# Retention states of sample batches: row groups of two batches, four 32-row updates, states by key halves

## The reference

```python
scores = jnp.einsum('bihd,bjhd->bhij', q, k) * mask[None]
inner = jnp.einsum('bhij,bjhe->bihe', scores, v)
cross = jnp.einsum('bihd,bhde->bihe', q, S) * q_dec[None, :, :, None]
S_new = (jnp.exp(log_g * C)[None, :, None, None] * S
         + jnp.einsum('bjhd,bjhe->bhde', k * k_dec[None, :, :, None], v))
return S_new, inner + cross
```

## Time and profile before

| | us |
|---|---|
| median of three timed runs (2913.4 to 2915.48) | 2915.39 |
| the profiled execution | 2908.85 |
| its span, first to last instruction | 2907.1 |
| TensorE busy | 2885.7 (99%) |
| VectorE busy | 1566.3 (54%) |
| ScalarE busy | 1121.1 (39%) |

### The profile page before, as it was taken

One profiled execution on the slowest core, in us unless ns is written; L12 is line 12 of the kernel. 1 busy time (PEld: TensorE's weight loads), 2 busy tenths in 40 slices (PEclk: granted clock), 3 DMA queues, 4 the chain that ended last, 5 costly groups with the idle time before them and its releaser, 6 DMA issues.

```text
span 2907.1 us, 57564 instructions
## 1 busy us (share of the span) xinstructions
PE 2885.7 (99%) x24818; PEld 2808.3 (97%) x24818; DVE 1566.3 (54%) x1695; ACT 1121.1 (39%) x1129; POOL 112.9 (4%) x144
## 2 busy tenths in 40 slices
PE   9999999999999999999999999999999999999998
PEld 9999999999999999898998999999999999999998
DVE  6444444444567566676765655465544444444444
ACT  5333333333334453444534644333433333333333
POOL 0000000000000002012020010000000000000000
PEclk9999999999999999999999999999999999999999
DMA  5444454444456543635436544555444444444444
GB/s 207 160 166 157 160 171 171 164 168 151 162 182 229 188 179 109 241 121 204 164 127 245 175 142 162 196 200 186 162 164 161 162 160 169 173 161 171 151 160 142
DMA packets 85461, 495.80 MB, mean 171 GB/s; under 512 B 10320, under 2 KB 10496, under 8 KB 44096
## 3 DMA queue, kind: packets, MB, share of 16 engines
q1 hardware_dynamic: 71424, 444.14, 43.2%
q0 software_dynamic: 9280, 32.70, 3.1%
q10 hardware_dynamic: 4608, 16.78, 1.4%
HBM read 462.78 MB, written 30.80 MB: 170 GB/s over the span
## 4 chain that ended last, share of the span: by engine, by line
PE 94%; DVE 3%; ACT 1%; DMA 1%; issue 0%; SPq 0%; DVEq 0%; ACTq 0%
PE psum L529 29%; PE psum L530 29%; PE psum L531 29%; PE psum L874 1%; PE psum L705 1%; DVE sb_w_lo L1486 1%; PE psum L695 1%; DVE sb_w_lo L1480 0%; PE psum L726 0%; DMA sb_raw<-in_w_wo 0%; PE psum L650 0%; ACT sb_w_hi L1066 0%; PE psum L884 0%; PE psum L887 0%; PE psum L945 0%
## 5 line engine op out<-in xcount | busy, mean ns | idle before, releaser
L529 PE MATMUL psum<-sb_h_hi,sb_w_hi 128*128 128x288 f32 x4384 | 1305.5, 298 | 3.0 <-DVE sb_w_lo L1480 1.5
L530 PE MATMUL psum<-sb_h_lo,sb_w_hi 128*128 128x288 f32 x4384 | 1294.2, 295 | 0.0
L531 PE MATMUL psum<-sb_h_hi,sb_w_lo 128*128 128x288 f32 x4384 | 1294.1, 295 | 0.0
L1486 DVE TENSOR_TENSOR sb_w_lo<-sb_raw,sb_w_hi 128x2048 fp32r<-128x2048 f32 (+1 forms) x348 | 712.4, 2047 | 724.5 <-ACT sb_w_hi L1066 721.5
L1066 ACT ACTIVATE sb_w_hi<-sb_raw 128x2048 fp32r<-128x2048 f32 (+1 forms) x349 | 600.2, 1720 | 1247.2 <-PE psum L531 1211.9
L529 PEld LDWEIGHTS psum<-sb_h_hi,sb_w_hi 128*128 128x128 f32 x4384 | 822.8, 188 | 19.7 <-issue 11.3
L530 PEld LDWEIGHTS psum<-sb_h_lo,sb_w_hi 128*128 128x128 f32 x4384 | 823.7, 188 | 2.5 <-issue 1.0
L531 PEld LDWEIGHTS psum<-sb_h_hi,sb_w_lo 128*128 128x128 f32 x4384 | 823.3, 188 | 0.0
L529 PE MATMUL psum<-sb_g_hi,sb_w_hi 128*128 128x288 f32 x1408 | 416.8, 296 | 0.7 <-DVE sb_w_lo L1486 0.5
L530 PE MATMUL psum<-sb_g_lo,sb_w_hi 128*128 128x288 f32 x1408 | 416.5, 296 | 0.0
L531 PE MATMUL psum<-sb_g_hi,sb_w_lo 128*128 128x288 f32 x1408 | 414.0, 294 | 0.0
(11 more groups left out here) (379 smaller groups left out, 2435.8 us busy)
## 6 DMA issues: line engine op xcount, KB each, us to landing
sb_raw<-in_gu SPq DMA_DIRECT2D x175, 1024.0 KB, 4.8
sb_raw<-in_down SPq DMA_DIRECT2D x128, 704.0 KB, 4.0
sb_raw<-in_w_mix SPq DMA_DIRECT2D x72, 1024.0 KB, 4.8
sb_raw<-in_w_gates SPq DMA_DIRECT2D x32, 1024.0 KB, 5.3
sb_s_ret<-in_s_ret POOLq DMA_DIRECT2D x32, 512.0 KB, 7.6
out_ret_s<-sb_s_ret ACTq DMA_DIRECT2D x32, 512.0 KB, 3.1
sb_raw<-in_w_ro SPq DMA_DIRECT2D x16, 1024.0 KB, 4.8
sb_raw<-in_w_out SPq DMA_DIRECT2D x16, 1024.0 KB, 4.8
```

The source lines that it names most:

```text
L529: pe.matmul(out, wh, xh, start=start, stop=False)
L530: pe.matmul(out, wh, xl, start=False, stop=False)
L531: return pe.matmul(out, wl, xh, start=False, stop=stop)
L1486: dve.tensor_tensor(w_lo[:, slot, 0:cols], raw[:, slot, 0:cols], w_hi[:, slot, 0:cols].bitcast(F32), ALU.subtract).then_inc(lo_made, 2)
```

## The change

The state slots no longer hold a batch each. A slot holds one key half of two batches, and the host permutes the states to fit. The sample's tokens are taken in four row groups of 32 rows: two batches of 4 tokens, four times over (three as high and low parts, the fourth zero). VectorE makes these repeated strips of values and keys first (`vs_rep`, `ks_rep`, step "gathered"), TensorE turns them by six ordinary turns of 128 columns instead of 18 narrow products, and factors by row (in `rc`) make high and low parts when they are copied out. An `update` is then four products of 32 rows, one for each row group and PSUM bank, for one key half of four batches; VectorE adds two batches' key half at once (128 x 1024). The output sums of the two halves are added by VectorE, so the fold is half as long. The sample's inner product takes split scores (`sc_3`) in one pass. The gaps have new weights. Left out in the diff: sizes and places of tiles, the names of steps, `cross` (its slot is now `2 * e + j // 2`), the splitting of `scores`, the waits' values, and the constants.

```diff
@@ -84,8 +84,8 @@
-RET_GAPS = (("turned", 2.6), ("scores", 4.2), ("kv_s0", 1.1), ("kv_s1", 1.1), ("kv_s2", 1.1), ("kv_s3", 1.4), ("kv1", 6.2),
-            ("kv_s4", 1.1), ("kv_s5", 1.1), ("kv_s6", 1.1), ("o_turned", 2.2), ("summed", 1.4), ("norm", 0.6))
+RET_GAPS = (("turned", 2.6), ("scores", 3.0), ("kv_s0", 0.8), ("kv_s1", 2.2), ("kv_s2", 2.2), ("kv1", 6.2),
+            ("kv_s3", 0.8), ("kv_s4", 2.2), ("kv_s5", 0.9), ("o_turned", 2.2), ("summed", 1.4), ("norm", 0.6))
@@ -663,10 +662,9 @@
+                after(ret_dve, RET_DVE, "gathered")
...
-                    for n in range(3):
-                        mm = pe.matmul(psum[n * NS:(n + 1) * NS, 5, m * P:(m + 1) * P], vg[:, 0, m, SEQ:T], ident[:, :],
-                                       start=True, stop=True)
+                    mm = transpose(psum[:, 5, m * P:(m + 1) * P], vs_rep[:, m, :])
@@ -676,43 +674,47 @@
-                    pe.matmul(psum[0:NS, 7, P:P + NS], qk[:, 2 + e, SEQ:T], qk[:, e, SEQ:T], start=(e == 0),
+                    pe.matmul(psum[:, 7, P:P + NS], ks_rep[:, e, :], qk[:, e, SEQ:T], start=(e == 0),
...
-                    for n in range(3):
-                        mm = pe.matmul(psum[n * NS:(n + 1) * NS, 4, e * P:(e + 1) * P], qk[:, 2 + e, SEQ:T], ident[:, :],
-                                       start=True, stop=True)
+                    mm = transpose(psum[:, 4, e * P:(e + 1) * P], ks_rep[:, e, :])
...
-                def update(half, bb, banks):
-                    for e in range(2):
-                        u = 2 * (bb - SLOTS * half) + e
-                        if u >= 3:
-                            pe.wait_ge(s_new, h * (2 * SB) + (2 * SLOTS * half + u - 2))
-                        step(pe.matmul(psum[:, banks[u % 3], :], k_own[:, bb % SLOTS, e * P:(e + 1) * P], v_3[:, :],
-                                       start=True, stop=True))
-                after(ret_dve, RET_DVE, "k_owned0")
+                def update(half, e):
+                    for j in range(SLOTS):
+                        rows = slice(j * NS, (j + 1) * NS)
+                        mm = pe.matmul(psum[:, 4 + j, :], k_own[rows, half, e * P:(e + 1) * P], v_3[rows, :], start=True, stop=True)
+                    step(mm)
+                after(ret_dve, RET_DVE, "masked")
...
-                for bb in range(SLOTS):
-                    update(0, bb, (6, 7, 4))
-                    weave(f"ret_kv_s{bb}")
-                pe.wait_ge(s_new, h * (2 * SB) + 2 * SLOTS - 2)
+                weave("ret_kv_s0")
...
+                after(ret_dve, RET_DVE, "k_owned")
+                pe.sem_inc(parted, 1)
+                update(0, 0)
+                weave("ret_kv_s1")
+                pe.wait_ge(s_new, h * SB + 2)
+                pe.sem_inc(parted, 1)
+                update(0, 1)
+                weave("ret_kv_s2")
+                pe.wait_ge(s_new, h * SB + 3)
@@ -729,21 +731,21 @@
+                pe.matmul(psum[0:NS, 6, :], sc_3[:, :], v_3[:, :], start=True, stop=False, skip_group_check=True)
+                cross(1, 6)
+                weave("ret_kv_s3")
+                after(ret_act, RET_ACT, "state1")
+                after(ret_dve, RET_DVE, "o_s_added")
...
-                pe.matmul(psum[0:NS, 6, :], scores[0:NS, 384:384 + NS], v_tok_s[:, :], start=True, stop=False,
-                          skip_group_check=True)
-                cross(1, 6)
-                after(ret_act, RET_ACT, "state1")
-                after(ret_dve, RET_DVE, "k_owned1")
-                for bb in range(SLOTS, SB):
-                    update(1, bb, (7, 4, 5))
-                    if bb < SB - 1:
-                        weave(f"ret_kv_s{bb}")
-                after(ret_act, RET_ACT, "o_s1")
+                update(1, 0)
+                weave("ret_kv_s4")
+                pe.wait_ge(s_new, h * SB + 6)
+                pe.sem_inc(parted, 1)
+                update(1, 1)
+                weave("ret_kv_s5")
+                pe.wait_ge(s_new, h * SB + 7)
...
-                    for half in range(2):
-                        mm = pe.matmul(psum[:, 6, m * NS:(m + 1) * NS], o_s[half][:, m * P:(m + 1) * P], rc[:, C_FOLD:RC],
-                                       start=(half == 0), stop=(half == 1), skip_group_check=True)
+                    mm = pe.matmul(psum[:, 4, m * NS:(m + 1) * NS], o_s[:, m * P:(m + 1) * P], rc[:, C_FOLD:RC], start=True, stop=True)
@@ -1262,24 +1264,28 @@
-                ch.do(act.activation(v_3[:, :], psum[0:3 * NS, 5, :], ACT.Copy), wait=False)
-                step(act.activation(v_tok_s[:, :], psum[0:NS, 5, :], ACT.Copy))
+                step(act.activation(v_3[:, :], psum[:, 5, :], ACT.Copy, scale=rc[:, C_V1:C_V1 + 1]))
...
-                ch.do(act.activation(k_s[:, :], psum[0:3 * NS, 4, 0:256], ACT.Copy, scale=rc[0:3 * NS, C_KD + 2:C_KD + 3]))
-                step(act.activation(k_3[:, :], k_s[:, :], ACT.Copy))
+                for half in range(2):
+                    ins = act.activation(k_own[:, half, :], psum[:, 4, 0:DK], ACT.Copy, scale=rc[:, C_KA0 + half:C_KA0 + half + 1])
+                    step(ins) if half else ch.do(ins, wait=False)
...
-                step(act.activation(o_s[0][:, :], psum[:, 5, :], ACT.Copy))
-                for bb in range(SLOTS):
-                    send(bb)
-                    weave(f"ret_kv_s{bb}")
+                step(act.activation(o_s[:, :], psum[:, 5, :], ACT.Copy))
+                weave("ret_kv_s0")
+                send(0)
+                send(1)
+                weave("ret_kv_s1")
+                send(2)
+                send(3)
+                weave("ret_kv_s2")
@@ -1287,12 +1293,13 @@
-                after(ret_pe, RET_PE, "cross1")
-                step(act.activation(o_s[1][:, :], psum[:, 6, :], ACT.Copy))
-                for bb in range(SLOTS, SB):
-                    if bb < SB - 1:
-                        weave(f"ret_kv_s{bb}")
-                    send(bb)
+                weave("ret_kv_s3")
+                weave("ret_kv_s4")
+                send(4)
+                send(5)
+                weave("ret_kv_s5")
+                send(6)
+                send(7)
@@ -1807,6 +1814,13 @@
+                mixed_in(dve, h, 7)
+                do(dve.tensor_copy(vs_rep[:, :, :].rearrange("p m (g c u) -> p m g c u", c=4, u=2 * ST),
+                                   vg[:, 0, :, SEQ:T].rearrange("p m (g u) -> p m g u", u=2 * ST).unsqueeze(3).broadcast_to(
+                                       [P, VT, 4, 4, 2 * ST])), wait=False)
+                step(dve.tensor_copy(ks_rep[:, :, :].rearrange("p m (g c u) -> p m g c u", c=4, u=2 * ST),
+                                     qk[:, 2:4, SEQ:T].rearrange("p m (g u) -> p m g u", u=2 * ST).unsqueeze(3).broadcast_to(
+                                         [P, 2, 4, 4, 2 * ST])))
@@ -1814,43 +1828,46 @@
-                step(dve.tensor_tensor(v_3[NS:2 * NS, :], psum[NS:2 * NS, 5, :], v_3[NS:2 * NS, :].bitcast(F32), ALU.subtract))
+                step(dve.scalar_tensor_tensor(out=v_3[:, :], in0=psum[:, 5, :], scalar=rc[:, C_V2:C_V2 + 1],
+                                              in1=v_3[:, :].bitcast(F32), op0=ALU.mult, op1=ALU.add))
...
-                rest = slice(2 * NS, 3 * NS)
-                step(dve.tensor_tensor(k_3[rest, :], k_s[rest, :], k_3[rest, :].bitcast(F32), ALU.subtract))
-                after(ret_dve, RET_DVE, "k_parts")
-                def own_keys(half):
-                    b = slice(SLOTS * half, SLOTS * (half + 1))
-                    step(dve.tensor_tensor(k_own[:, :, :], k_3[:, :].bitcast(F32).unsqueeze(1).broadcast_to([3 * NS, SLOTS, DK]),
-                                           own[0:3 * NS, b].unsqueeze(2).broadcast_to([3 * NS, SLOTS, DK]), ALU.mult))
-                own_keys(0)
+                for half in range(2):
+                    ins = dve.scalar_tensor_tensor(out=k_own[:, half, :], in0=psum[:, 4, 0:DK],
+                                                   scalar=rc[:, C_KB0 + half:C_KB0 + half + 1],
+                                                   in1=k_own[:, half, :].bitcast(F32), op0=ALU.mult, op1=ALU.add)
+                    step(ins) if half else do(ins, wait=False)
...
-                def state_s(half, bb, banks):
-                    for e in range(2):
-                        after(ret_pe, RET_PE, f"kv_s{bb}" + "eo"[e])
-                        u = 2 * (bb - SLOTS * half) + e
-                        dve.scalar_tensor_tensor(out=s_ret[:, bb % SLOTS, e, :], in0=s_ret[:, bb % SLOTS, e, :],
-                                                 scalar=rc[:, C_KD + 3:C_KD + 4], in1=psum[:, banks[u % 3], :], op0=ALU.mult,
-                                                 op1=ALU.add).then_inc(s_new, 1)
-                for bb in range(SLOTS):
-                    state_s(0, bb, (6, 7, 4))
-                    weave(f"ret_kv_s{bb}")
-                own_keys(1)
+                def states(half, e):
+                    after(ret_pe, RET_PE, f"kv_s{half}{e}")
+                    for pr in range(2):
```

(50 more changed lines are left out.)

33 lines of the change are left out of this document (16 added, 17 removed).

## The result

The change makes the kernel slower: 2930.47 us (median of 5 runs, 2930.21 to 2931.77) against 2914.14 for the kernel before on the same chip (5 runs), a ratio of 1.0056, 95% interval [1.0042, 1.0071], +16.3. The forecast was 2936.5 with a range of 2924 to 2945. The profiled execution has a span of 2928.8, +21.7 over the 2907.1 of before; forecast for that comparison was +21.2.

What follows compares the result with a forecast made beforehand. TensorE, busy 99% of the span, was taken as the bound. Savings −17.0, holes +25.2, state waits +4.2 and clock +8.8 gave +21.2, 2930.0 profiled; with 6.5 to the median, 2936.5, range 2924 to 2945.

Steps and rivals of the forecast that it cites:

- value turns: TensorE, start of each head: four plain turns replace 12 products of 32 columns, 0.44 against 1.00, −0.56 a head.
- scores: TensorE, scores in each head: four instructions and two turns, 0.66 against 0.68, no change.
- updates: TensorE, state updates: four groups on four strips at 0.40 replace 16 products, 1.6 against 3.7, −2.1 a head.
- sample's scores times values: TensorE, the sample's own scores times values: two passes of 0.97 become one of 0.235, −0.74 a head.
- fold: TensorE, fold after the last updates: 16 instructions, 1.87 long, become 8, −0.85 a head.
- holes: TensorE waits for VectorE's copies before its turns: 6.0 in heads two to four, 7.1 in the first, +25.2.
- waits for states: TensorE waits for VectorE's state operations: 0.1 after a half's first group, 1.3 before the fold in three heads, +4.2 together.
- clock behind the holes: TensorE at half rate after each hole: 2.2 lost per hole, bounds 0 and 2.8, +8.8 for four.
- The third rival: Second cross products: state stores and loads come late, up to 1.2 a head, 2941.3; chance 0.08.
- From the profiled execution to the median: Whole kernel: the timed median lies 6.5 above the profiled execution; added to the change, 2930.0 profiled becomes 2936.6.
- The rival of an undisturbed clock: TensorE behind the holes: the clock stays up, or falls in one head only, 8.8 less, 2927.8; chance 0.22.

Runs made afterwards that it cites:

- double groups: The changed kernel with every group of four updates issued twice into the same banks, 16 groups more: 2935.98 us, one run.
- filled holes: The changed kernel with 46 (first head 54) turns of a constant matrix before each wait for the copies: 2928.8 us, ratio 1.0051.
- the version with the pieces from another gap: The change with copies moved ahead and woven pieces taken from before the first cross products, put before fold and second cross products: 2905.34 us, ratio 0.9968.

## Why the prediction was right, and where its terms were off

The side, the place and the mechanism came as forecast: four holes before the turns of the repeated values, released by VectorE's copy of the keys, a fall of the clock behind each, a wait before the fold in heads one to three. Term by term, in the profiled executions, four heads together:

| term | forecast | measured |
|---|---|---|
| value turns | −2.2 | −3.0 |
| scores | 0 | −1.0 |
| updates | −8.4 | −4.9 |
| sample's scores times values | −3.0 | −3.0 |
| fold | −3.4 | −3.1 |
| holes | +25.2 | +23.9 |
| waits for states | +4.2 | +3.7 |
| clock behind the holes | +8.8 | +7.2 |
| falls elsewhere | 0 | about +3 |

The first eight add to +19.8; from the first turn to the end of the fold the four heads are longer by 5.60, 4.96, 5.36 and 3.79, together 19.7. With two falls in the RWKV parts, 1.5 in the one measured above, that is within 1 of the +21.7; the kernel before has a wait of 0.81 in the RWKV part of its second head (at 1299.80) that the change's trace lacks. That forecast and measurement of the profiled executions (+21.2 and +21.7) lie so close is partly luck: the updates save 3.5 less than said, turns, scores, holes and clock together cost some 4.7 less, and the falls elsewhere, about 3, weren't forecast at all.

- **Updates.** This is the worst term. The group itself is 0.43 where 0.40 was said. Missed was the neighbourhood: each group starts 0.09 late behind its woven product, the second woven product behind it 0.11 late, and there is such a step behind the cross products too, where a pair followed directly before. With that the four groups of the second head stand for 2.7, where the sixteen products had 3.95: 1.2 a head are saved, not 2.1. The double groups bear out that four strips cost one product and the rest comes once.
- **Holes.** From the start of the first copy to the end of the second VectorE needs 0.62, not 1.04: the copies run at twice the rate of the q products, near the lower bound of the forecast.
- **The clock.** 2.2 a hole was said, 1.5 to 2.0 came. That the clock falls is shown by the windows, and that the slow products are its doing by the filled holes. One row was misread, without effect on the sum: at the end of the kernel before, TensorE's last product (`L568`, 2894.61 and 1.24 long) ends at 2895.85, so that TensorE had been idle for some 2.6 when the clock fell, and a hole of 6 is a little over twice that, not three times.
- **Turns and scores.** With the 32-column products their switches of 0.09 go as well, which the rows showed and the sum left out.
- **States.** The wait before the fold is 1.0 between starts (1.3 said), three times. The third rival came in one head: in the third, the second cross products waited 0.65 for a load. Its 8.1 for a load was the median of the first head; in the second head of the kernel before it is 6.7.
- **From the profiled execution to the median.** This step failed, and it is nearly all of the 6 us between 2936.5 and 2930.5. The prediction added the 6.5 by which the timed runs of before exceed its profile to the change as well. The executions of before show what those 6.5 are, by their mean clock and not by a trace: falls of the clock which its profiled execution was spared. The changed kernel's executions lie at 0.992 or 0.993 all alike, profile included, so there was nothing to add. Why the change has so even a number of falls, and the kernel before hasn't, stays open; the filled holes show only that with the clock kept up there the timed executions still have a mean clock of 0.995 or 0.996.

The rival of an undisturbed clock (2927.8) lies 2.7 from the median, nearer than the forecast. It isn't what happened: the clock fell at all four holes.

## What to carry to other kernels

Before new work is put ahead of a wait, look where the engine that makes it stands at that moment: here 0.54 of copies at the head of the next part cost 29 us, and the same copies 11 us earlier in idle time cost nothing. Cost a packed group with the switches on both of its sides, by the start of what follows it. And before a difference between a profiled and a timed run is carried over to a changed kernel, ask what it is made of; the mean granted clock that stands beside each run told it here.

## What the runs showed of the hardware that was not expected

- The granted clock falls to half for 3 us and more (0.50 from 1331.00 to 1333.00 in the change) with TensorE never idle, behind 64 products of 8 columns; at most once a head in these traces, and not in every execution. The Trainium skill ("TensorE: Matmul & The Clock Gate", part 1) ties the fall to an idle TensorE; these rows show one without idle time.
- Idle times of 5.53, 2.78 and 6.64 all brought the fall; 0.51 behind the filling turns didn't. Between these the length alone doesn't decide: in the version with the pieces from another gap an idle time of 1.90 brought it (granted clock 0.79 from 1000.00 to 1002.00, then 0.50), while 2.13, 2.36 and 2.44 in the same trace didn't (1.00 in the windows behind them).
- Four passes of 512 columns on four 32-row strips cost what one costs (0.24, by the double groups). Once per group or double group 0.19 come on top, and the steps ahead of it and behind it are 0.09 and 0.11 longer than between woven products.
- A copy of 512 elements a partition keeps VectorE 0.34 (1179.13 to 1179.47) with a source that repeats each group of values four times; the q products needed 0.34 for 256.
